# First output projection in seven products of quarters, with feed-forward weights, modulations and one delta product moved

## The chip, the cores and the metric

The kernel runs on one core of one Trainium2 chip. Its time is the device time of one execution in microseconds (us), and the median of three runs is given. TensorE (PE) multiplies matrices into PSUM, VectorE (DVE), ScalarE (ACT) and GpSimd (POOL) work on elements, and SP issues the DMA transfers. Everything is fp32. An engine works through its own instructions in order, and the engines wait for each other by semaphores.

## The reference

768 tokens (256 context, 512 latent) of 1024 features go through two layers of a diffusion transformer with different mixers, and then the latent tokens through a second block with a delta-rule mixer, latent attention and experts. The parts that the change touches, cut:

```python
for l in range(2):
    m = split((silu(c) @ mod_w[l] + mod_b[l]), 6)              # modulations
    h = rms(x, norm_pre_mix[l]) * (1 + m[1]) + m[0]
    o = even_mixer(h) if l == 0 else odd_mixer(h)              # l = 0: gated linear attention, softmax attention
    x = x + m[2] * rms(o @ w_out, norm_post_mix[l])            # output projection: out0, out1
    h = rms(x, norm_pre_ffn[l]) * (1 + m[4]) + m[3]
    x = x + m[5] * rms((silu(h @ w_gate[l]) * (h @ w_up[l])) @ w_down[l], norm_post_ffn[l])
# layer 1 is computed for the 512 latent tokens only; D_FF = 2816
```

## The kernel before

The features or tokens lie on 128 partitions; there are 6 tiles of 128 tokens (TILES), the first two context. The stages follow one another, each a block of instructions for all engines with tensors and semaphores of its own: opening, `even_mixer` (gla), `even_attention` (att), `closing` (out0), `gate_up` and `down` (ffn0), `odd_mixer` (hgrn), `closing` (out1), `gate_up` and `down` (ffn1), `delta_mixer` (dn), and the later ones up to the experts. A stage's instructions are issued only when the engine has left the stage ahead. An `Ahead` is a small buffer that an earlier stage's SP fills for a later one.

**`closing`** multiplies hT (features by tokens, 8 tiles of 128 features) with the output weights in the plain form: for each of 2 blocks of 512 columns and each of 6 token tiles, 8 products of 128x512 that add up in one bank (L633, L651). Behind the second block's products the tile two places back, which ScalarE and VectorE have normalised, is turned by 8 transpositions (L601), and its modulation is taken from PSUM by ScalarE (L685) and VectorE (L758).

**`down`** multiplies in seven products for eight (Strassen's, in Winograd's form), on quarters: a couple of token tiles by a pair of feature tiles of the weights (`lo`, `hi`) by two halves of the columns. In a step j TensorE issues the products 1, 6, 2, 7, 5, 4, 3 (L1235), each of 128x512, each into its own bank, over all steps of a couple. GpSimd makes two sums of each step's weights (L1298, L1299) and VectorE two more (L1323, L1325) and, for two steps at once, four sums of the operands (L1312 to L1317). At a couple's end VectorE collects the seven banks into the two tiles (L1329, seven adds), and in the steps of the next couple these are squared (ScalarE L1264), gated (L1353), added to the residual x (L1361), squared again (L1273), normalised (L1373), turned (TensorE L1206) and taken (L1283, L1380). The weights come by SP in steps of 1 MB into three homes. It has 11 steps a couple, `STEPS`.

**`gate_up`** does the same with quarters of 2816 hidden features, in units (gate and up by turns): products L960, GpSimd's sums L1018, L1019, L1023, VectorE's L1040, L1042, L1049, L1051.

**`even_attention`** runs 24 units of softmax attention. Twenty modulations (chunks of `mod_w`, 64 narrow products on TensorE, L2127, bias on VectorE, L2330) are spread over it, four of them ahead of the first scores (L2164), the rest at marks in the loop (`mod_at`). SP streams their weights in two homes (L2079) and stores all results at the end (L2089). The row sums of squares of q and k are products with a constant `att_two`, brought by DMA (L2136).

**`delta_mixer`** runs 10 periods of 6 chunks n; in period p the inputs of head p are projected (L3324) while chunks of earlier heads go through the recurrence. z0 (L3373) multiplies masked matrices dn_W with the identity, ScalarE copies the result to Z (L3676) and VectorE adds (`right`, L3775).

## Time and profile before

| | us |
|---|---|
| median of 3 runs (4270.95, 4272.61, 4286.95) | 4272.61 |
| the profiled execution's own time / its span | 4270.7 / 4268.9 |
| attention stage (att) | 307.5 to 504.9 |
| first output projection (out0) | 504.9 to 602.0 |
| gate and up, layer 0 / down, layer 0 | 602.0 to 1008.2 / 1008.2 to 1234.3 |
| hgrn, out1 | 1234.3 to 1781.2 |
| gate and up, layer 1 / down, layer 1 | 1781.2 to 2080.3 / 2080.3 to 2240.3 |
| delta mixer and later | 2240.3 to 4268.9 |

A stage's start is read from the first DMA issue of its SP in the timeline. In the timeline a row is: start, duration, engine, line, operation, what it writes <- what it reads, shapes, number of instructions put together, and in brackets how long the engine had been idle before and what ended it. A fp32 product is two records, so "x24" of products are 12 instructions. PEld is the load of the stationary operand beside the products. A wait row says which engine's instruction waited for which, total us, how often, and the longest. Idle time of an engine other than TensorE matters only if TensorE, or SP's loads, wait for it. PEclk is the granted clock of TensorE, 1.00 is full.

### The profile page before, as it was taken

How to read it: one execution, taken by the hardware profiler on the slowest of the kernel's cores; microseconds unless marked ns; L12 is line 12 of the kernel's file. 1: busy time of each engine (PE TensorE's matmuls, PEld its weight loads, DVE VectorE, ACT ScalarE, POOL GpSimd, SP SyncE). 2: the span in 40 equal slices, each digit the busy share in tenths (PEclk: the TensorE clock that was granted, in tenths of full speed). 3: DMA queues.
4: the chain of work that ended last, by engine and by line, in shares of the span. 5: the costliest groups of instructions: out<-in, count | busy, mean ns of one | idle time of the engine just before them, and what ended most of it. 6: DMA issues, size and time to landing. Idle time of an engine off the chain costs nothing. (4 is left out here: it accounts for less than half of the span.)

```text
span 4268.9 us, 51405 instructions
## 1 busy us (share of the span) xinstructions
PE 3946.4 (92%) x20867; PEld 2419.5 (57%) x20867; DVE 1673.3 (39%) x3130; ACT 852.4 (20%) x1663; POOL 690.8 (16%) x513
## 2 busy tenths in 40 slices
PE   7997889999999999899989899989998898999988
PEld 4665545554458666588646666767654445443333
DVE  2346442234764554533473555543124224111111
ACT  3224320000121332200013333321123211000000
POOL 0003212223420111122332232310002200000000
PEclk8998999999999999999998999999999998999999
DMA  4107511113532110253332010004200224999999
GB/s 172 40 24 270 194 40 59 59 60 114 173 108 60 30 45 32 107 217 139 133 128 54 21 31 23 21 34 139 81 1 1 116 79 169 406 421 422 422 421 369
DMA packets 323409, 580.12 MB, mean 136 GB/s; under 512 B 58876, under 2 KB 189404, under 8 KB 322536
## 3 DMA queue, kind: packets, MB, share of 16 engines
q1 hardware_dynamic: 323176, 576.84, 36.9%
q8 instruction: 168, 2.75, 0.3%
q14 instruction: 65, 0.53, 0.0%
HBM read 566.15 MB, written 10.63 MB: 135 GB/s over the span
## 5 line engine op out<-in xcount | busy, mean ns | idle before, releaser
L3324 PE MATMUL dn_ps<-room,dn_w 128*128 128x512 f32 (+1 forms) x616 | 229.6, 526 | 5.2 <-DVE dn_qx L3862 3.5
L960 PE MATMUL ffn_up_ps<-room,ffn_up_w 128*128 128x384 f32 (+1 forms) x704 | 208.8, 440 | 12.7 <-DMA ffn_up_w<-in_ffn_w_gate 12.7
L960 PE MATMUL ffn_up_ps<-ffn_up_t,room 128*128 128x384 f32 (+1 forms) x704 | 204.0, 433 | 1.2 <-DVE room L1040 1.2
L960 PE MATMUL ffn_up_ps<-room 128*128 128x384 f32 (+1 forms) x704 | 203.9, 432 | 0.0
L4870 PE MATMUL experts_ps<-experts_ring,experts_xs 128*64 128x512 f32 (+1 forms) x768 | 162.2, 573 | 25.3 <-DMA experts_ring<-in_w_up 25.3
L960 PEld LDWEIGHTS ffn_up_ps<-room,ffn_up_w 128*128 128x128 f32 x704 | 134.9, 193 | 71.9 <-DMA ffn_up_w<-in_ffn_w_gate 13.5
L3324 PEld LDWEIGHTS dn_ps<-room,dn_w 128*128 128x128 f32 x616 | 117.0, 195 | 96.0 <-issue 82.4
L2634 PE MATMUL hgrn_ps<-room,hgrn_w 128*128 128x512 f32 x372 | 170.3, 593 | 0.9 <-DVE hgrn_v L2888 0.9
L4870 PE MATMUL experts_ps<-experts_ring,room 128*64 128x512 f32 (+1 forms) x768 | 160.9, 569 | 8.7 <-DMA experts_ring<-in_w_up 8.1
L960 PEld LDWEIGHTS ffn_up_ps<-ffn_up_t,room 128*128 128x128 f32 x704 | 133.8, 190 | 57.4 <-DVE room L1040 1.9
L960 PEld LDWEIGHTS ffn_up_ps<-room 128*128 128x128 f32 x704 | 133.8, 190 | 55.7
L1235 PE MATMUL ffn_down_ps<-ffn_down_w_sums,ffn_down_hid_sums 128*128 128x512 f32 x330 | 161.8, 599 | 2.3 <-DVE ffn_down_w_sums L1323 2.3
L1047 DVE TENSOR_TENSOR room<-ffn_up_ps,room 128x384 f32<-128x384 f32 (+1 forms) x154 | 73.4, 489 | 222.2 <-PE ffn_up_ps L960 222.2
L4964 DVE TENSOR_TENSOR x_sb<-x_sb,experts_ps 128x512 f32<-128x512 f32 x56 | 38.5, 688 | 297.9 <-PE experts_ps L4805 297.9
L4920 PE MATMUL experts_ps<-experts_ring,experts_hidT 128*64 128x512 f32 x616 | 135.5, 594 | 10.2 <-issue 6.0
L4870 PEld LDWEIGHTS experts_ps<-experts_ring,experts_xs 128*64 128x64 f32 x768 | 58.6, 140 | 130.0 <-issue 126.7
L651 PE MATMUL out_ps<-out_w,room 128*128 128x512 f32 x296 | 131.0, 601 | 0.8 <-ACT room L699 0.8
L1235 PE MATMUL ffn_down_ps<-ffn_down_w,ffn_hid 128*128 128x512 f32 x220 | 116.5, 612 | 15.3 <-DMA ffn_down_w<-in_ffn_w_down 14.5
L1018 POOL TENSOR_TENSOR room<-ffn_up_w 128x512 f32<-128x512 f32 x44 | 56.7, 1288 | 440.3 <-PE ffn_up_ps L960 233.3
L1323 DVE TENSOR_TENSOR ffn_down_w_sums<-ffn_down_w,ffn_down_w_sums 128x512 f32<-128x512 f32 x55 | 82.0, 1490 | 95.7 <-POOL ffn_down_w_sums L1298 95.7
L4870 PEld LDWEIGHTS experts_ps<-experts_ring,room 128*64 128x64 f32 x768 | 54.5, 139 | 109.8 <-issue 108.2
L1235 PEld LDWEIGHTS ffn_down_ps<-ffn_down_w_sums,ffn_down_hid_sums 128*128 128x128 f32 x330 | 63.4, 193 | 84.4 <-issue 83.0
(665 smaller groups left out, 7176.7 us busy)
## 6 DMA issues: line engine op xcount, KB each, us to landing
experts_ring<-in_w_gate SPq DMA_DIRECT2D x128, 704.0 KB, 14.2
experts_ring<-in_w_up SPq DMA_DIRECT2D x128, 704.0 KB, 17.4
experts_ring<-in_w_down SPq DMA_DIRECT2D x160, 512.0 KB, 13.0
ffn_down_w<-in_ffn_w_down SPq DMA_DIRECT2D x55, 1024.0 KB, 4.9
att_wm<-in_mod_w SPq DMA_DIRECT2D x20, 2048.0 KB, 9.3
ffn_up_wm<-in_ada_w SPq DMA_DIRECT2D x12, 2048.0 KB, 12.5
ffn_up_w<-in_ffn_w_up SPq DMA_DIRECT2D x22, 1024.0 KB, 7.6
ffn_up_w<-in_ffn_w_gate SPq DMA_DIRECT2D x20, 1024.0 KB, 5.4
```

The source lines that it names most:

```text
L651: mm = nc.tensor.matmul(ps[:, u % BANKS, 0:wd], xT[:, k, t * P:(t + 1) * P], wt[:, j % ring, k, 0:wd], start=k == 0, stop=k == kt - 1)
L960: mm = nc.tensor.matmul(result(n, p), lhs[:, k, :], rhs[:, k, :], start=k == 0, stop=k == half - 1)
L1018: nc.gpsimd.tensor_tensor(s[:, 0, :, :], quarter(n, 1, lo), quarter(n, 1, hi), ALU.add).then_inc(S["s1_done"], 1)
L1047: nc.vector.tensor_tensor(kept(n, to), result(n, p), kept(n, q), ALU.add).then_inc(done, 1)
L1235: mm = nc.tensor.matmul(result(p, prod), lhs, rhs, start=j == 0, stop=j == STEPS - 1)
L1323: nc.vector.tensor_tensor(t[:, 1, :], hi[:, right], t[:, 0, :], ALU.subtract).then_inc(S["t2_done"], 1)
L2634: mm = nc.tensor.matmul(ps[:, bank, :], weights(j, k)[:, piece * P:(piece + 1) * P], hT[:, k, CTX:], start=k == 0, stop=k == KD - 1)
L3324: mm = nc.tensor.matmul(out, ahead.tile[:, k, :] if k < by_ahead else wt[:, h % 2, piece, k, :], hT[:, k, tok], start=k == 0, stop=k == KD ...
L4870: mm = nc.tensor.matmul(ps[out_rows, 3 * n + c, 0:b - a], xs_now[:, j, at:at + SLOTS], ring[:, w_at + a:w_at + b], start=j == 0, stop=j == ...
L4920: mm = nc.tensor.matmul(ps[out_rows, 6 + half, :], hidT[:, f, out_rows], ring[:, w_at:w_at + 512], start=f == 0, stop=f == FT - 1)
L4964: nc.vector.tensor_tensor(dst, dst, ps[:, bank, :], ALU.add).then_inc(S["scatter_out"], 1)
```

## The change

Four parts.

1. **out0** is computed by `down` instead of `closing`, with 4 steps a couple (`short`): couples (0,3), (1,4), (2,5). The weights, 4 MB, are streamed once for each couple, three DMAs a step. Of the first step only the low half is brought by the stage ahead. Turnings stand at other steps, and VectorE's schedule in a couple is a new one.
2. **Feed-forward weights.** `front` (the first gate weights) is loaded at the end of out0 and out1, and `gate_up` brings the first two steps of `down` (`next_load`, waited for as `early_in`) once its last block but one is multiplied. For this the homes of the weights are shared between `gate_up` and `down`.
3. **Attention.** Three modulations instead of four open the stage: two ahead of the first scores, one behind the second. One more stands at the end, after the last pair's values. The constant is made by VectorE, and the reductions for the scan's norm stand ahead of VectorE's wait for the key's factors.
4. **Delta mixer.** z0 and the copy of it move from the end of a period (n = 5) to the start of the next, behind `out_of`; z0 and two sums of squares use bank 5.

```diff
+    STEPS = hid.shape[1] // 2
+    short = STEPS < 10
+    if short:
+        turn_after = {(2, 1): (0, 0), (2, 5): (0, 1), (3, 2): (1, 0), (3, 5): (1, 1)}
+    GATES_AT = 3 if short else 8
...
+                        if beside and (j, at_order) in turn_after:
+                            which, part = turn_after[j, at_order]
+                            turn(p, beside[which], part)
...
+                    if short and beside:
+                        one, other = beside
+                        if j == 0:
+                            mean_y(one)
+                            gated(one)
+                            mean_y(other)
+                            residual(one)
+                            gated(other)
+                        elif j == 1:
+                            mean_x(one)
+                            residual(other)
+                            normed(one)
+                        elif j == 2:
+                            mean_x(other)
+                            normed(other)
+                        else:
+                            take(p, one)
+                            take(p, other)
+                        continue
...
-    closing(nc, "out0", hT, KD, out0_jobs, x, mix, hT, ident,
-            (mods[0], 2, I["norm_post_mix"][0]), (I["norm_pre_ffn"][0], mods[0], 3, 4), ahead=out0)
+            down(nc, "out0", hT, None, x, mix, hT, ident, (mods[0], 2, I["norm_post_mix"][0]), (I["norm_pre_ffn"][0], mods[0], 3, 4), front.load, small[:, :],
+                 [out0_w[:, n, :] for n in range(3)], out0_w[:, 3, :], [], 0, fetch=out0_fetch, ahead=out0)
...
 # gate_up
         def weights_here(eng, n):
             if n == 0:
-                eng.wait_ge(S["lo_in"], 16)
-            eng.wait_ge(S["w_in"][2 * ((n // 2) % 2) + n % 2], 16 * (n // 4 + 1))
+                eng.wait_ge(front.sem, 16)
+            else:
+                eng.wait_ge(S["w_in"][n % 4], 16 * (n // 4 + (1 if n % 4 else 0)))
...
+            sp.wait_ge(S["product"], 7 * 2 * (blocks - 1))
+            next_load(sp)
...
 # even_attention
-    OPENING, LOOP = 4, 4
+    OPENING, LOOP = 3, 4
+    OPENING_BANKS = (3, 6)
...
-        return (0, 1, 3, 4) if j + 1 < PAIRS else (0, 1, 2, 3)
+        return (0, 1, 3, 4) if j + 1 < PAIRS else (0, 1, 2, 3, 4)
...
-            for m in range(OPENING):
-                modulated(m, m)
+            for m, bank in enumerate(OPENING_BANKS):
+                modulated(m, bank)
...
+                if u == 0:
+                    modulated(len(OPENING_BANKS), OTHER)
...
 # delta_mixer, TensorE, ScalarE, VectorE
+                else:
+                    side("z0", hi)
...
-                elif n == 5:
-                    side("z0", hp)
...
+                    if hi is not None:
+                        act.wait_ge(S["side"], side_n["z0", hi])
+                        nc.scalar.copy(Z[:, :, :], blocks(5)).then_inc(S["z_start"], 1)
...
+                if n == 0:
+                    right(0, hi)
...
-                    right(0, hp)
```

TensorE's order in out0, before: the plain products, with turnings behind the last blocks (out0_ps is the stage's PSUM, cst holds the identity).

```order
L651 MATMUL out0_ps<-out0_w,room 128x512 x60
L601 MATMUL out0_ps<-cst,room 128x128 x8
L651 MATMUL out0_ps<-out0_w,room 128x512 x8
L601 MATMUL out0_ps<-cst,room 128x128 x8
L651 MATMUL out0_ps<-out0_w,room 128x512 x8
L601 MATMUL out0_ps<-cst,room 128x128 x8
L651 MATMUL out0_ps<-out0_w,room 128x512 x8
L601 MATMUL out0_ps<-cst,room 128x128 x24
```

After, in steps three and four of the second couple (out_w_sums holds the sums of weights and, as the stationary operand, those of hT):

```order
L1259 MATMUL out_ps<-out_w 128x512
L1259 MATMUL out_ps<-out_w,room 128x512
L1259 MATMUL out_ps<-out_w_sums,out_w 128x512
L1229 MATMUL out_ps<-cst,room 128x128 x4
L1259 MATMUL out_ps<-out_w,room 128x512
L1259 MATMUL out_ps<-out_w_sums,out_w 128x512 x2
L1259 MATMUL out_ps<-out_w_sums,room 128x512
L1229 MATMUL out_ps<-cst,room 128x128 x4
L1259 MATMUL out_ps<-out_w 128x512
L1259 MATMUL out_ps<-out_w,room 128x512
L1259 MATMUL out_ps<-out_w_sums,out_w 128x512
```

A tile is now turned in two halves between single products, and the products before and behind need sums of the same step.

TensorE's order at the seam of two periods of the delta mixer, before:

```order
L3404 MATMUL dn_ps<-dn_LT,dn_Y 64x64 x12
L3433 MATMUL dn_ps<-room,dn_T 128x128 x2
L3373 MATMUL dn_ps<-cst,dn_W 64x64 x12
L3461 MATMUL dn_ps<-dn_state,dn_qT 128x256
L3463 MATMUL dn_ps<-room,dn_qk 128x128 x2
```

After:

```order
L3479 MATMUL dn_ps<-dn_LT,dn_Y 64x64 x12
L3508 MATMUL dn_ps<-room,dn_T 128x128 x2
L3536 MATMUL dn_ps<-dn_state,dn_qT 128x256
L3538 MATMUL dn_ps<-room,dn_qk 128x128 x2
L3536 MATMUL dn_ps<-dn_state,dn_qT 128x256
L3538 MATMUL dn_ps<-room,dn_qk 128x128 x2
L3448 MATMUL dn_ps<-cst,dn_W 64x64 x12
L3399 MATMUL dn_ps<-room,dn_w 128x512 x8
```

z0 (dn_W) has moved behind the four products of the outputs and stands right ahead of the projection.

## Rows read from the trace of the kernel before

**Rows 1.** Page, part 1: busy us (share of span) and instructions by engine.

```profile
PE 3946.4 (92%) x20867; PEld 2419.5 (57%) x20867; DVE 1673.3 (39%) x3130; ACT 852.4 (20%) x1663; POOL 690.8 (16%) x513
```

**Rows 2.** TensorE's waits to 2300: for what; us in total, times, longest.

```profile
PE ffn_down_ps L1235 <- DMA ffn_down_w<-in_ffn_w_down: 14.5, 2, 7.4
...
PE ffn_up_ps L960 <- DMA ffn_up_w<-in_ffn_w_gate: 12.7, 2, 6.4
...
PE att_ps L2127 <- DMA att_wm<-in_mod_w: 7.8, 2, 6.1
```

**Rows 3.** TensorE's waits in the delta mixer, 2240 to 3000.

```profile
PE dn_ps L3373 <- DVE dn_W L3846: 15.1, 8, 4.5
...
PE dn_ps L3324 <- DVE dn_qx L3862: 3.5, 6, 0.6
```

**Rows 4.** Timeline, z0: start, us, engine, line, operation, out<-in, count, [idle <-releaser].

```profile
2301.20 1.55 PE L3373 MATMUL dn_ps<-cst,dn_W 64*64 64x64 f32 x24 [3.36 <-DVE dn_W L3846]
```

**Rows 5.** Timeline of the attention stage's opening.

```profile
330.20 3.79 SPq L2079 DMA_DIRECT2D att_wm<-in_mod_w  x2
...
331.45 1.93 PE L2127 MATMUL att_ps<-att_wm,conditions 128*2 128x128 f32 x64
...
332.94 0.69 DVE L2344 TENSOR_TENSOR even_raw<-att_tmp 128x512 f32<-128x512 f32 x1
...
339.52 3.59 PE L2127 MATMUL att_ps<-att_wm,conditions 128*2 128x128 f32 x64 [6.14 <-DMA att_wm<-in_mod_w]
...
349.55 2.85 PE L2164 MATMUL att_ps<-even_raw 64*128 64x256 f32 x16 [1.36 <-issue]
...
356.44 1.12 PE L2196 MATMUL att_ps<-cst,att_probs 128*128 128x128 f32 x4 [4.04 <-DVE att_probs L2405]
```

**Rows 6.** Timeline of the attention stage's end.

```profile
495.95 3.97 SPq L2089 DMA_DIRECT2D mod<-att_mod  x8
...
496.07 5.37 PE L2213 MATMUL att_ps<-att_pT,even_av 128*64 128x512 f32 x24 [0.81 <-DVE att_mod L2330]
```

**Rows 7.** SP's waits, 300 to 620.

```profile
SPq L44 <- DMA mod<-att_mod: 1.4, 1, 1.4
```

**Rows 8.** Windows: from:to, us, busy us (instructions) by engine, PEclk, DMA share, GB/s.

```profile
505.00:602.00 97.00, 89.15 (x240) 42.41 (x240) 34.08 (x82) 27.33 (x73) 0.00 (x0) 0.97 0.20 55
1024.00:1076.00 52.00, 52.00 (x123) 23.06 (x122) 29.93 (x36) 0.00 (x0) 22.32 (x18) 1.00 0.61 211
1081.00:1147.10 66.10, 65.95 (x166) 29.98 (x165) 48.27 (x71) 9.65 (x22) 28.17 (x21) 1.00 0.50 166
```

**Rows 9.** Timeline of the first down projection's start.

```profile
1008.27 0.42 DVE L1312 TENSOR_TENSOR ffn_down_hid_sums<-ffn_hid 128x256 f32<-128x256 f32 x1 [1.82 <-PEq L47]
...
1013.23 2.07 PE L1235 MATMUL ffn_down_ps<-ffn_down_w,ffn_hid 128*128 128x512 f32 x2 [7.44 <-DMA ffn_down_w<-in_ffn_w_down]
...
1014.48 1.26 POOL L1299 TENSOR_TENSOR ffn_down_w_sums<-ffn_down_w 128x512 f32<-128x512 f32 x1
1014.55 1.74 DVE L1323 TENSOR_TENSOR ffn_down_w_sums<-ffn_down_w,ffn_down_w_sums 128x512 f32<-128x512 f32 x1 [4.72 <-POOL ffn_down_w_sums L1298]
...
1016.43 2.05 PE L1235 MATMUL ffn_down_ps<-ffn_down_w_sums,ffn_down_hid_sums 128*128 128x512 f32 x2 [1.13 <-DVE ffn_down_w_sums L1323]
...
1023.56 1.02 PE L1235 MATMUL ffn_down_ps<-ffn_down_w,ffn_hid 128*128 128x512 f32 x2
```

**Rows 10.** The same, later: an operand sum beside GpSimd.

```profile
1102.63 1.43 DVE L1312 TENSOR_TENSOR ffn_down_hid_sums<-ffn_hid 128x256 f32<-128x256 f32 x1
```

**Rows 11.** The same stage's end.

```profile
1228.71 3.48 PE L1206 MATMUL ffn_down_ps<-cst,room 128*128 128x128 f32 x16 [8.27 <-DVE room L1373]
```

**Rows 12.** Timeline of the first gate-and-up stage's start.

```profile
602.01 1.76 DVE L1049 TENSOR_TENSOR ffn_up_t<-room 128x1536 f32<-128x1536 f32 x1 [1.14 <-PEq L47]
...
605.83 5.22 PE L960 MATMUL ffn_up_ps<-room,ffn_up_w 128*128 128x384 f32 x8 [6.37 <-DMA ffn_up_w<-in_ffn_w_gate]
...
610.89 2.74 PE L960 MATMUL ffn_up_ps<-ffn_up_t,room 128*128 128x384 f32 x8
```

More of the change, by code:

```diff
@@ L1081, in _, with down @@
                         ins.then_inc(S["mod_out"], 1)
-def down(nc, tag, hid, w, x, y, hT, ident, gate, norm, then, small, tile0=0, before=None):
+def down(nc, tag, hid, w, x, y, hT, ident, gate, norm, then, small, raw, hsum, early_in, tile0=0, before=None, fetch=None, ahead=None):
     mod_g, gate_at, gain = gate
     gain_n, mod_n, shift_at, scale_at = norm
-    STEPS = DFF // P // 2
+    STEPS = hid.shape[1] // 2
[3 more added lines that the diff above has]
+    else:
+        turn_after = {(6, 6): (0, 0), (7, 6): (0, 1), (8, 6): (1, 0), (9, 6): (1, 1)}
+    GATES_AT = 3 if short else 8
     half = D // 2
@@ L1163, in tokens, with pieces, low, high @@
             return slice((t - tile0) * P, (t - tile0 + 1) * P)
+        def pieces(n):
+            j = n % STEPS
+            if fetch is None:
+                return [(raw[n % RAW], w.rearrange("(k p) n -> p k n", p=P)[:, j::STEPS, :])]
+            return fetch(raw[n % RAW], j, 1 if ahead and n == 0 else 0)
+        arrived, so_far = [], [0] * RAW
+        for n in range(n_pairs * STEPS):
+            if n >= len(early_in):
+                so_far[n % RAW] += 16 * len(pieces(n))
+            arrived.append(so_far[n % RAW])
+        def low(n):
+            return ahead.tile[:, 0, :] if ahead and n == 0 else raw[n % RAW][:, 0, :]
+        def high(n):
+            return raw[n % RAW][:, 1, :]
         @block.sync
         def _(sp):
-            v = w.rearrange("(k p) n -> p k n", p=P)
             def weights(n):
@@ L1192, in weights_here @@
         def weights_here(eng, n):
-            eng.wait_ge(S["w_in"][n % RAW], 16 * (n // RAW + 1))
+            if n < len(early_in):
+                eng.wait_ge(early_in[n], 16)
+            else:
+                eng.wait_ge(S["w_in"][n % RAW], arrived[n])
+                if ahead and n == 0:
+                    eng.wait_ge(ahead.sem, 16)
         @block.tensor
@@ L2047, in even_attention @@
         n_mod = len(chunks)
-        assert n_mod == OPENING + LOOP * PAIRS
+        assert n_mod == OPENING + sum(len(mod_at(j)) for j in range(PAIRS))
         wm = sb("wm", 2, KD, 512)
@@ L2344, in rope @@
                 nc.vector.tensor_tensor(lat, tmp[:, 0, :], tmp[:, 1, :], ALU.add).then_inc(S["roped"], 1)
+            for a in range(2):
+                for b in range(2):
+                    nc.vector.memset(two[a * DH:(a + 1) * DH, b:b + 1], 1.0 if a == b else 0.0).then_inc(S["two_set"], 1)
             dve.wait_ge(S["const_in"], CONSTS)
@@ L3048, in first_block, with out0_fetch @@
     gla = Ahead(first, loaded[0], I["even_w_in"][0].rearrange(by_feature, p=P)[:, :, E_Z:E_Z + 2 * GLA_RANK])
-    out0_jobs = columns(I["even_w_out"][0], range(TILES), rows=pair_rows)
-    out0 = Ahead(first, loaded[1], out0_jobs[0][0][0][0][1][:, 0:2, 0:512])
+    out0_rows = pair_rows(I["even_w_out"][0])
+    (_, scan_rows), = out0_rows[0]
+    out0 = Ahead(first, loaded[1], scan_rows[:, 0:1, :])
+    def out0_fetch(dst, j, have):
+        return [(dst[parts, half:half + 1, :], rows[:, j:j + 1, :]) for half in range(have, 2) for parts, rows in out0_rows[half]]
     hgrn = AheadPieces(first, loaded[0], [I["odd_w_in"][0].rearrange(by_feature, p=P)[:, 0:2, i * D:i * D + P] for i in range(3)])
@@ L3372, in side @@
                         for side, rows in enumerate(sides_of):
[L3373 removed]
+                            mm = nc.tensor.matmul(block_of(5, side, c), W[rows, h % 2, c, :], ident[rows, rows], start=True, stop=True)
                 mm.then_inc(S["side"], 1)
```

154 lines of the change are left out of this document (81 added, 73 removed).

## The prediction

> **What bounds the kernel now.** I read the busy times of the page first. TensorE works 3946 of 4269 us [rows 1], so the other engines matter only where TensorE waits for them, and the time can fall in two ways only: less work for TensorE, or fewer of its waits. Then I read its waits up to the end of the first block [rows 2]: 14.5 us for the first weights of the two down projections, 12.7 us for those of the two gate-and-up projections, and 7.8 us for the modulation weights of the attention stage. In the delta mixer, 15.1 us stand at one small product, called z0 below [rows 3]. The change aims at each of these. The experts behind all this run at the rate of their weights, but their loads wait for the stages ahead, so what is won or lost earlier reaches the end in full. What has to be asked of each wait is what TensorE would wait for next.
>
> **Attention stage, opening.** Now four modulations stand ahead of the first scores. Two ran without a wait; the other two stand right before the scores and wait 7.8 us for their weights [rows 2], the first for 6.14 us after a load issued at 330.20. The scores come at 349.55, and the first transposition of probabilities at 356.44, so the chain maximum, exponential, sum, normalisation takes 6.9 us [rows 5]. After the change only the two modulations without a wait stand ahead of the scores. The last rope on VectorE ends at 333.6 [rows 5], and six reductions that stood behind it now stand ahead of it, in a stretch where VectorE waited. So the scores start at about 334. GpSimd's gating now lies beside the chain, for which I add 2 us. The first transposition comes at about 334 + 6.9 + 2 = 342.9, which is 13.5 us earlier (bounds 12 and 15.7). The third modulation stands behind the scores, and its weights land at 339.5 as now, just ahead of that.
>
> **Attention stage, end.** One modulation of 64 products is moved to the very end, behind the products of the last values. Those start at 496.07 and take 5.37 us [rows 6], so it starts at 501.4. It needs 0.7 for its bank, 1.9 for itself (the 64 products at 331.45 took that [rows 5]) and 1.2 for VectorE to add the bias: 505.2. Only then may SP store all modulations. It does so now at 495.95 in 3.97 us, beside those products, and waits 1.4 us for their landing [rows 6, 7]. After: 505.2 + 0.5 + 3.97 + 1.4 = 511.1, where the next stage begins at 504.9 now. That is 6.2 us later. The store had been covered by the products, and that cover is gone. Together the attention stage gives 13.5 - 6.2 = **7.3 us** back.
>
> **First output projection.** Now the stage takes 97.0 us, with 96 matmul instructions (each two records of the trace) and TensorE busy for 89.2 [rows 8]. After: 3 couples x 4 steps x 7 = 84. One step of seven lasts 66.1 / 11 = 6.01 us, from the second couple of the first down projection, which runs the same function and in which TensorE is busy for 65.95 of 66.10 us [rows 8]. So the products take 84 x 0.858 = 72.1 us, 10.3 less than 96 of them. But the function has a start and an end. The first down projection takes 226.1 us for 33 steps, so 226.1 - 33 x 6.01 = 27.8 us are overhead: the DMA wait (5 us from the stage's start), the wait for the first sums (3.2 us), the slow clock of its start (the first product takes 2.07 us where it takes 1.02 later), the transpositions of four tiles inside, and at the end 8.3 us until the last couple is normalised and 5.6 more to turn it [rows 9, 11]. That gives 72.1 + 27.8 = 99.9, already 3 us more than now. The old form turned its tiles beside products of other tiles.
>
> Then VectorE. In the down projection it has 11 steps to finish a couple of tiles beside the next, here 4. In the 52.0 us ahead of the first collection it is busy 29.93 us with sums alone: 29.93 / 52.0 x 6.01 = 3.46 us a step. In the 66.1 us of a couple with normalisation it is busy 48.27, so the rest is 48.27 - 11 x 3.46 = 10.2 us [rows 8]. Here a couple has 4 x 3.46 + 10.2 = 24.0 us of VectorE beside 4 x 6.01 + 1.7 = 25.7 us of TensorE. It is 93% full, and most of its work is a chain with ScalarE and GpSimd, where it can't be packed. An operation that has to wait for GpSimd is long: the same sum of operands takes 0.42 us alone and 1.43 us beside GpSimd [rows 9, 10]. I laid the operations of couples two and three out one behind the other with these durations. The product of the third step waits 3.3 us for its weight sums, which stand behind the mean, gate and residual of the tiles; the first turning waits 2.2 us for the normalised tile, the second 2.7 us for VectorE to take the first, and 0.5 is left at a step. The second couple comes to 8.6 us of waits, the third to 5.4. At the end the last collection begins behind the second take: 4.9 us more, of which about 1 is won back, since no long wait stands ahead. Sum: 99.9 + 8.6 + 5.4 + 4.9 - 1 = 117.8, so **+20.8 us** (bounds +3 if every wait is hidden, +30 if the clock falls in them).
>
> The rule on the two engines can be weighed. The weight sum at 1014.55 is recorded with 1.74 us beside GpSimd's of 1014.48, which ends at 1015.74 [rows 9]. The Trainium skill, in "SBUF — State Buffer", section "Who interferes with whom", says that a VectorE operation with two SBUF inputs and a GpSimd operation that reads SBUF exclude each other, and the one that issues second waits until the first is done. By that rule 0.69 us behind 1015.74 would end at 1016.4, and the trace has 1016.3, so it agrees. Without the rule, with 0.68 us for each of these, VectorE would have some 4 us less a couple, and the stage would come to about 108 us.
>
> **Weights ahead of the feed-forwards.** The waits for DMA fall away, but the product right behind is bound by sums, not by weights. In the first gate-and-up stage the weights come at 605.83, and the first product on a sum at 610.89, though the stage begins at 602.0: 8.9 us [rows 12]. VectorE's first operand sum, which ran alone under that wait, takes 1.76 us [rows 12]. After, two of these and the weight sums, 1.3 us and more each, start together and take turns: 6.3 us if VectorE comes first, 10.0 if GpSimd does, 8.15 between them. So 0.75 us less, and I give the second such stage, with four tiles for six, the same: **-1.5** (bounds -12.7, if the sums cost nothing, and +4). For the down projections the first sum is used 8.2 us after the start (1008.27 to 1016.43). Now four operand sums of 0.42 us run while the weights are awaited [rows 9]; after they take turns with GpSimd at 1.43 [rows 10], and the product comes after about 6.8 us with a DMA that has long landed. Later steps gain no more, since the slow clock at the start stays. I take **-1.5** for both (bounds -14.5 and 0). The early loads themselves run beside products in stages where the DMA engines have room.
>
> **Delta mixer.** z0 waits for VectorE's masks eight times, 15.1 us in all [rows 3]; the first two periods hold 3.4 [rows 4] and 4.5 of it, and there nothing else is ready, so they stay. The other six are 7.3 us. Behind it now come the outputs of the period before, then z0, then the projection, whose eight products of 0.86 hide ScalarE's copy and VectorE's first use. The sums of squares move to a bank of their own, which frees the projection of a wait of 3.5 us [rows 3], and the copy of z0 does so for 1.1. Less 0.7 for one wait that the last period gains: 11.2. Since such waits partly come back at the next chain (neighbours of z0 wait in the same period), I take **-10** (bounds -4 and -16).
>
> **Sum.** Against the profiled execution's own time of 4270.7 us: -7.3 + 20.8 - 1.5 - 1.5 - 10 = +0.5, so 4271. The median of the runs is 2 us higher, which I leave out. Forecast: **4271 us, no change** (about 0.5%, 21 us either way, is what a measurement of this kernel can tell from none).
>
> **Rivals.**
> A. The weights ahead pay in full: TensorE's 12.7 and 14.5 us go, since one of the two summing engines gets through first and the clock recovers earlier. Then 4271 - 24 = 4247. For it: those rows name the DMA and nothing else. Against: sums that start with the stage take 6.3 us at best.
> B. VectorE's work in the short stage is hidden better than laid out, by a luckier order of turns: out0 at 104 us, 4271 - 14 = 4257. With A it would be 4233. For it: VectorE is at 93%, not over 100.
> C. Slower. Place: couples two and three of the first output projection. VectorE's chain, not TensorE, sets each step, and TensorE's clock falls in the gaps as it does at the start of the down projection. One slow stretch in each couple costs 5 us, ten us of products at 2.07 for 1.02 us [rows 9]. A couple takes 25.7 + 7 = 32.7 us in my sum; one of 39 costs 13 more over both: 4271 + 10 + 13 = 4294. It decides from a couple of 38 us on.
> D. Attention and delta mixer give nothing, because the waits move to the next chain: 4271 + 17 = 4288.
>
> **How the numbers follow.** Chances: forecast 0.45, B 0.17, A (with or without B) 0.20, D 0.10, C 0.08. Range: 4244 to 4290, which leaves out most of C, a little of D and A with B in full. Faster (below 4251): A and some of B, 0.22. Slower (above 4292): C and the tail of D, 0.09. No change: 0.69.
>
> **What would show it.** In the profile after: the stage from the attention's last product to the first gate-and-up product at 115 to 121 us, TensorE waiting there on VectorE's weight sums and on its taken tiles, and a last wait of 12 us ahead of the last turning; the first transposition of probabilities 13 us earlier and the store of the modulations behind the last product; no DMA wait at the four feed-forward stages but 6 to 10 us to the first product on a sum; z0 without a wait in six of eight periods. I am wrong if out0 stays under 108 us, or if the four starts take under 4 us.

## The result: 0.5% slower, where no change was forecast

The changed kernel takes 4300.6 us (median of 5 runs, 4295.24 to 4303.42), the kernel before, run as often, 4273.9. The ratio is 1.0053, with a 95% interval of 1.0043 to 1.0064. The profiled execution's span is 4299.6 us at a mean clock of 0.954 (before 4268.9 at 0.960), 30.7 us more. My range ended at 4290.

A stage lasts from its SP's first DMA issue to the next stage's. All tables below are read that way from the timeline of SP.

| stage | before | after | difference | forecast |
|---|---|---|---|---|
| up to attention | 307.4 | 306.8 | -0.6 | |
| attention | 197.4 | 193.5 | -3.9 | -7.3 |
| out0 | 97.1 | 127.5 | +30.4 | +20.8 |
| gate and up 0 / down 0 | 406.3 / 226.1 | 410.1 / 225.3 | +3.8 / -0.8 | -0.75 / -0.75 |
| hgrn / out1 | 465.6 / 81.3 | 465.5 / 81.5 | -0.1 / +0.2 | |
| gate and up 1 / down 1 | 299.1 / 160.0 | 299.7 / 159.1 | +0.6 / -0.9 | -0.75 / -0.75 |
| delta mixer | 663.0 | 660.6 | -2.4 | -10 |
| its projections / mla | 119.7 / 359.7 | 119.5 / 362.9 | -0.2 / +3.2 | |
| mix / wo to the end | 126.9 / 759.3 | 125.8 / 761.7 | -1.1 / +2.4 | |

### The profile page after: what moved, and what is told of

Its sections match the earlier page's. It is cut to its first block and busy times, and to the rows that moved or that the text cites. A ratio compares the mean times of both kernels' runs of the same rounds, so it can differ in the third digit from the quotient of the medians.

```text
span 4299.6 us, 51462 instructions
## 1 busy us (share of the span) xinstructions
PE 3965.8 (92%) x20843; PEld 2425.4 (56%) x20843; DVE 1732.6 (40%) x3191; ACT 852.5 (20%) x1654; POOL 727.7 (17%) x537
## 5 line engine op out<-in xcount | busy, mean ns | idle before, releaser
L961 PE MATMUL ffn_up_ps<-ffn_up_t,room 128*128 128x384 f32 (+1 forms) x704 | 208.4, 440 | 10.2 <-DVE room L1037 10.2
L1259 PE MATMUL ffn_down_ps<-ffn_down_w_sums,ffn_w 128*128 128x512 f32 x330 | 163.2, 604 | 10.8 <-DVE ffn_down_w_sums L1347 10.8
L961 PE MATMUL ffn_up_ps<-room,ffn_w 128*128 128x384 f32 (+1 forms) x512 | 148.8, 434 | 0.0
L961 PEld LDWEIGHTS ffn_up_ps<-room,ffn_w 128*128 128x128 f32 x512 | 97.0, 190 | 41.2 <-issue 1.1
L1259 PEld LDWEIGHTS ffn_down_ps<-ffn_down_w_sums,ffn_w 128*128 128x128 f32 x330 | 63.9, 194 | 92.2 <-issue 90.8
L3772 POOL TENSOR_TENSOR dn_LT<-dn_W,cst 128x384 f32<-128x384 f32 x48 | 47.9, 997 | 376.9 <-DVE dn_W L3858 337.0
L4996 PEld LDWEIGHTS experts_ps<-experts_ring,experts_hidT 128*64 128x64 f32 x616 | 51.0, 138 | 89.0 <-issue 89.0
L1715 PE MATMUL gla_ps<-gla_w,room 128*128 128x384 f32 x288 | 100.0, 501 | 0.0
L2682 PEld LDWEIGHTS hgrn_ps<-room,hgrn_w 128*128 128x128 f32 x372 | 66.0, 191 | 59.8 <-issue 59.5
## 6 DMA issues: line engine op xcount, KB each, us to landing
ffn_up_wm<-in_ada_w SPq DMA_DIRECT2D x12, 2048.0 KB, 12.5
```

The costliest lines, as they stand in the source:

```text
L961: mm = nc.tensor.matmul(result(n, p), lhs[:, k, :], rhs[:, k, :], start=k == 0, stop=k == half - 1)
L1259: mm = nc.tensor.matmul(result(p, prod), lhs, rhs, start=j == 0, stop=j == STEPS - 1)
L1715: mm = nc.tensor.matmul(ps[:, bank, 0:wd], hT[:, k, t * P:(t + 1) * P], wt[:, s, k, 0:wd], start=k == 0, stop=k == KD - 1)
L2682: mm = nc.tensor.matmul(ps[:, bank, :], weights(j, k)[:, piece * P:(piece + 1) * P], hT[:, k, CTX:], start=k == 0, stop=k == KD - 1)
L3772: nc.gpsimd.tensor_tensor(LT[:, :, :], W[:, h % 2, :, :], small(SMALL_HALVES + n + 1), ALU.mult).then_inc(S["lt_done"], 1)
L4996: mm = nc.tensor.matmul(ps[out_rows, 6 + half, :], hidT[:, f, out_rows], ring[:, w_at:w_at + 512], start=f == 0, stop=f == FT - 1)
```

## The profile after

Waits of TensorE up to 2300 in the changed kernel (engine, tile, line, awaited: total us, times, longest). They answer [rows 2].

```profile
PE out_ps L1229 <- DVE room L1397: 12.4, 1, 12.4
...
PE ffn_down_ps L1259 <- DVE ffn_down_w_sums L1347: 10.8, 2, 5.4
PE ffn_up_ps L961 <- DVE room L1037: 10.2, 2, 6.7
PE out_ps L1259 <- DMA out_w<-in_even_w_out: 9.6, 1, 9.6
...
PE out_ps L1259 <- DVE room L1353: 4.3, 1, 4.3
...
PE out_ps L1229 <- DVE room L1404: 2.8, 1, 2.8
```

No row is left of the 27 us of waiting for the weights of the feed-forwards. In their place stand 10.8 and 10.2 us for sums by VectorE (L1347, L1037). out0 has waits that it did not have before: 12.4 at its end, 9.6 at its start (4.6 of it inside the stage, which begins at 500.22), 4.3 for the first collection, 2.8 for a taken tile.

The start of the first gate-and-up stage after the change, from the timeline, answers [rows 12]:

```profile
627.79 2.87 DVE L1046 TENSOR_TENSOR ffn_up_t<-room 128x1536 f32<-128x1536 f32 x1 [0.74 <-PEq L47]
627.79 2.82 PE L961 MATMUL ffn_up_ps<-room,ffn_front 128*128 128x384 f32 x8 [2.15 <-PEq L47]
...
631.74 4.93 POOL L1020 TENSOR_TENSOR room<-room 128x1536 f32<-128x1536 f32 x1
633.32 3.90 DVE L1037 TENSOR_TENSOR room<-room,ffn_front 128x512 f32<-128x512 f32 x1
...
637.27 5.49 PE L961 MATMUL ffn_up_ps<-ffn_up_t,room 128*128 128x384 f32 x8 [6.66 <-DVE room L1037]
```

The weights are there, and product 1 runs at once. Then TensorE waits 6.66 us. VectorE's two operand sums and s2 (L1037), and GpSimd's t3 (L1020, 4.93 us) take turns, and product 6 comes 9.5 us after the start, later than the 8.9 us of before. It then takes 5.49 us, where the same product took 2.74 before [rows 12]: the clock is still down.

out0, the second couple and the last turning, from the timeline of the changed kernel:

```profile
535.40 4.49 DVE L1424 TENSOR_TENSOR out_gate<-out_gate,room 128x1024 f32<-128x1024 f32 x2
536.57 2.24 POOL L1323 TENSOR_TENSOR out_w_sums<-out_w 128x512 f32<-128x512 f32 x1
539.92 4.53 DVE L1353 TENSOR_TENSOR room<-out_ps,room 128x512 f32<-128x512 f32 x7
...
540.67 1.77 PE L1259 MATMUL out_ps<-out_w,room 128*128 128x512 f32 x2 [4.30 <-DVE room L1353]
...
542.24 2.97 PE L1259 MATMUL out_ps<-out_w_sums,out_w 128*128 128x512 f32 x4
...
558.54 1.09 PE L1229 MATMUL out_ps<-cst,room 128*128 128x128 f32 x4 [3.59 <-issue]
```

```profile
570.68 0.68 PE L1229 MATMUL out_ps<-cst,room 128*128 128x128 f32 x4 [2.76 <-DVE room L1404]
...
595.77 1.09 PE L1229 MATMUL out_ps<-cst,room 128*128 128x128 f32 x4 [3.59 <-issue]
...
622.00 3.65 PE L1229 MATMUL out_ps<-cst,room 128*128 128x128 f32 x16 [12.37 <-DVE room L1397]
```

The two products of gates and gain (L1424) take 4.49 us beside GpSimd and stand ahead of the collection (L1353, 539.92), so TensorE waits 4.30 us at 540.67. Behind it two records take 1.77 and four 2.97 us, where two take 1.02 and four 1.88 at full clock. The same happens behind 558.54 (a wait of 3.59), 570.68 (2.76) and 595.77 (3.59).

## Experiments

Twelve kernels were run. A ratio is to the kernel before on the same chip. Where a kernel ran only once (early_late, warm, sched, fill, end_first, before_again), I go by the lengths of the stages. hgrn, which no edit touches, took 465.3 to 465.6 us in 11 of 14 traces and 464.9 to 466.9 in all. Other stages vary more without an edit: p34_only has 301.5 and 227.3 us in the second gate-and-up and the first down stage, where the kernel before had 299.1 and 226.1. Attention varies by 5 us from trace to trace, and the delta mixer once by 3.7 (fill). So a difference of 1 or 2 us between two stages says little by itself.

| stage | p34_only | p2_only | p1_off | p34_off | early_late | warm | sched | fill | end_first | best1 | best2 |
|---|---|---|---|---|---|---|---|---|---|---|---|
| attention | 191.2 | 202.1 | 192.0 | 200.0 | 189.7 | 190.4 | 191.9 | 192.9 | 194.7 | 194.9 | 192.4 |
| out0 | 98.6 | 97.1 | 99.7 | 128.3 | 123.4 | 126.4 | 114.5 | 124.2 | 112.1 | 99.7 | 99.8 |
| gate, up 0 | 405.7 | 409.2 | 409.6 | 410.1 | 405.6 | 407.1 | 403.9 | 403.9 | 403.9 | 407.5 | 403.8 |
| down 0 | 227.3 | 224.9 | 225.1 | 225.3 | 224.7 | 222.8 | 224.4 | 225.4 | 223.8 | 222.8 | 222.8 |
| gate, up 1 | 301.5 | 299.3 | 299.3 | 299.7 | 295.9 | 298.0 | 295.9 | 295.9 | 295.9 | 297.4 | 295.6 |
| down 1 | 160.5 | 159.4 | 159.7 | 159.1 | 159.2 | 158.2 | 159.2 | 159.4 | 159.2 | 157.2 | 157.2 |
| delta mixer | 659.4 | 663.6 | 660.1 | 663.6 | 660.7 | 659.7 | 660.6 | 664.3 | 660.6 | 661.1 | 659.5 |
| mla | 363.0 | 363.0 | 363.0 | 363.0 | 362.8 | 362.9 | 362.9 | 362.8 | 362.8 | 363.0 | 363.1 |

### The parts one by one

**p1_off**: out0 in the plain form again.

```diff
-            down(nc, "out0", hT, None, x, mix, hT, ident, ...)
+        closing(nc, "out0", hT, KD, out0_jobs, x, mix, hT, ident, ..., ahead=out0, then=front.load)
```

> The changed kernel with the first output projection in the plain form again; the other three parts stay. Theory T (the loss is out0's own, 127.5 us against 97.1, and the other parts add up to about zero): out0 takes 97 us again, the kernel 4270 us, the gate-and-up stage behind it still 3 to 4 us longer than before. Rival R1 (the loss lies partly in what out0 leaves behind, the slow clock with which the next stage starts): out0 gives back 30, and the next stage 4 more, so 4266 us.

Measured: 4269.6 us (10 runs, 4266.41 to 4275.54), ratio to before 0.9984 (0.9974 to 0.9993). out0 takes 99.7 us. The loss of the whole change is out0's, 28 us by the stages and 31 by the medians. The gate-and-up stage behind it stays at 409.6, so R1 falls: that stage's loss is its own.

**p34_off**: attention and delta mixer as before, the rest as changed (both functions taken whole from the kernel before).

> The changed kernel with the attention stage and the delta mixer as before. Theory T (by the stages of the two traces, attention is worth 3.6 us and the delta mixer 2.4): the kernel takes 4306 us, with an attention stage of 197.4 and a delta mixer of 663. Rival R2 (both are worth what was forecast, 7 and 10, and something else in the changed kernel hid it): 4316 us or more.

Measured: 4309.2 us (4 runs, 4304.94 to 4312.97), 1.0073 (1.0056 to 1.009), with 200.0 and 663.6 us in the two stages. Both parts gain. The time lies between the two expectations, nearer to theory T's 4306.

**p34_only**: the kernel before with the two functions of the change.

> The kernel before with only the changed attention stage and the changed delta mixer. Theory T (attention is worth about 7 us, as 199.5 against 192 in the mean of the traces so far, the delta mixer 2.5): 4276.5 - 9.5 = 4267 us. It also tells where the 3.3 us of latent attention (mla, 359.7 in both traces of before, 362.9 in all six of changed kernels, at the same waits) come from: 359.7 here if they belong to the weights ahead, 362.9 if they belong to the delta mixer or to any shift of the program. Rival R2 (the attention gain is run-to-run variation of that stage): 4272 us or more.

Measured: 4267.0 us (10 runs, 4260.3 to 4273.4), 0.9977 (0.9968 to 0.9986), where theory T had 4267; it had counted on 9.5 us less than the kernel before, and on this chip it is 7.4 less (4274.4). Attention is 191.2. Over all traces, the old form takes 197.4, 201.7, 202.1 and 200.0, the new one 189.7 to 194.9 (ten traces), so some 8 us; the trace after the change, with 193.5, showed less than the usual gain. mla takes 363.0 here too.

**p2_only**: the kernel before with the feed-forward weights ahead.

> The kernel before with only the feed-forward weights ahead (with GpSimd's order as in the change). By the stages of p1_off: gate-and-up +3.4 and -0.5, out0 up to +2.6, down -1 and +0.5, mla +3.2 if it belongs to it. Theory T (the DMA wait is exchanged for a wait on sums and a longer slow clock, so the 27 us of DMA waits give nothing): 4276.5 + 3 to 8, about 4282 us. Rival A of the prediction (the waits for DMA come through in full): 4250 us.

Measured: 4278.4 us (10 runs, 4273.85 to 4282.36), 1.0007 (0.9998 to 1.0016). 27 us of DMA waits are gone from the trace and nothing is gained; the interval holds 1. Rival A falls. The four stages stand at 409.2, 224.9, 299.3 and 159.4: together 1.3 us more than before.

### What stands behind the starts

**early_late**: two edits in stages apart.

```diff
-    GATES_AT = 3 if short else 8
+    GATES_AT = 2 if short else 8
...
             weight_sums(0)
-            pool.wait_ge(S["t1_done"], 1)
+            pool.wait_ge(S["s2_done"], 1)
             nc.gpsimd.tensor_tensor(t3, b22, b12, ALU.subtract)
```

> The changed kernel with two edits in stages that do not touch. In out0 VectorE multiplies the gates one step earlier, at the third step of the first couple. In both gate-and-up stages GpSimd makes the operand sum t3 only behind VectorE's first weight sum s2. Theory T (VectorE was late for the first collection because of the gates, and s2 because it took turns with t3): TensorE's wait of 4.3 us in out0 ahead of the second couple goes and out0 falls from 127.5 to about 123; the first product on a sum of the gate-and-up stage comes 6 us after the start where it came after 9.5, and the stage is 3 us shorter. Rival R3 (collection and s2 are late for the many sums as such): out0 stays within 1 us of 127.5, and the wait only moves to the turnings; the gate-and-up stage stays at 410.

Measured: out0 123.4 (-4.1), the two gate-and-up stages 405.6 and 295.9 (-4.5 and -3.8). TensorE's wait ahead of product 6:

```profile
627.00 4.54 PE L961 MATMUL ffn_up_ps<-ffn_up_t,room 128*128 128x384 f32 x8 [1.85 <-DVE room L1037]
```

Product 6 comes 6.25 us after the start of 620.75, with 1.85 us of waiting for s2 left in the row. One wait, moved on GpSimd, brings 8.3 us in two stages. So theory T holds for both edits: s2 was late because it took turns with t3, and the gates stood ahead of the collection.

**warm**: product 1 repeated at the starts.

```diff
+                        for again in range(3 if n == 0 and prod == 1 else 0):
+                            nc.tensor.matmul(result(p, prod), lhs, rhs, start=True, stop=True)
                         mm = nc.tensor.matmul(result(p, prod), lhs, rhs, start=j == 0, stop=j == STEPS - 1)
```

> The changed kernel with more products at three starts, results thrown away: in the gate-and-up stages the first unit's product 1 is made three times, in the down stages and out0 the first step's product 1 four times. It tests whether the slow clock behind the starts comes from TensorE's idle gap of 5 to 7 us there. Theory T (the gap costs twice, once itself and once as products at half the clock behind it; with TensorE busy in the gap the clock is full when the sums are there): product 6 of the first gate-and-up stage takes 2.7 us instead of 5.5, and the stage is 3 to 5 us shorter, each down stage 2 to 4 us shorter. Rival R4 (the clock comes back only some time after the stage's start, whatever TensorE does): the stages keep their length within 1 us, or get longer by the added products.

Measured, against the changed kernel: down 222.8 and 158.2 (-2.5, -0.9), gate and up 407.1 and 298.0 (-3.0, -1.7), out0 126.4 (-1.1). The start of the first down stage, from TensorE's timeline, in the changed kernel and in warm:

```profile
1037.91 1.10 PE L1259 MATMUL ffn_down_ps<-ffn_w,ffn_hid 128*128 128x512 f32 x2 [2.60 <-PEq L47]
...
1044.38 2.05 PE L1259 MATMUL ffn_down_ps<-ffn_down_w_sums,ffn_w 128*128 128x512 f32 x2 [5.38 <-DVE ffn_down_w_sums L1347]
...
1046.22 1.92 PE L1259 MATMUL ffn_down_ps<-ffn_w,ffn_hid 128*128 128x512 f32 x2
...
1047.93 2.71 PE L1259 MATMUL ffn_down_ps<-ffn_down_w_sums,ffn_w 128*128 128x512 f32 x4
```

```profile
1031.20 2.81 PE L1263 MATMUL ffn_down_ps<-ffn_w,ffn_hid 128*128 128x512 f32 x6 [2.60 <-PEq L47]
1033.85 1.02 PE L1264 MATMUL ffn_down_ps<-ffn_w,ffn_hid 128*128 128x512 f32 x2
1037.68 1.10 PE L1264 MATMUL ffn_down_ps<-ffn_down_w_sums,ffn_w 128*128 128x512 f32 x2 [2.81 <-DVE ffn_down_w_sums L1352]
1038.62 1.02 PE L1264 MATMUL ffn_down_ps<-ffn_w,ffn_hid 128*128 128x512 f32 x2
1039.48 1.88 PE L1264 MATMUL ffn_down_ps<-ffn_down_w_sums,ffn_w 128*128 128x512 f32 x4
```

In the changed kernel TensorE waits 5.38 us after one product, and the next take 2.05, 1.92 and 2.71 us. In warm it makes three more products, whose result nobody uses, waits 2.81 us, and the same ones take 1.10, 1.02 and 1.88. The wait was paid twice. R4 falls at this start, which is 2.5 us shorter. The 0.9 us of the second down stage would fit R4 too; in best1 and best2, with the same repeated products, that stage takes 157.2, 1.9 less than in the changed kernel. In the gate-and-up stage product 6 starts at 633.59, 9.5 us after the start, as in the changed kernel, and takes 2.85 for 5.49 us, as theory T had it.

### Inside out0

**sched**: early_late, and in out0

```diff
-        turn_after = {(2, 1): (0, 0), (2, 5): (0, 1), (3, 2): (1, 0), (3, 5): (1, 1)}
+        turn_after = {(2, 3): (0, 0), (2, 6): (0, 1), (3, 2): (1, 0), (3, 5): (1, 1)}
...
+                    if short and beside and j == 3:
+                        take(p, beside[0])
                     if n + 1 < n_pairs * STEPS:
```

> As early_late, and in out0 the first turning of a couple stands two products later, and VectorE takes the first turned tile ahead of the next couple's sums, behind which it had stood. Theory T (the waits of 2.8, 2.8 and 0.7 us come from the place of the turning and from that order on VectorE, and each of the long ones costs another 1.5 to 1.8 us of slow clock): the waits go down to about 1, the slow stretches behind them go too, and out0 takes 111 to 116 us instead of 123.4. Rival R3 (VectorE has too much to do in a short couple, so that the lateness only moves): 121 or more.

Measured: out0 114.5 us. Its longest waits from 530 on:

```profile
551.28 1.76 PE L1259 MATMUL out_ps<-out_w_sums,out_w 128*128 128x512 f32 x2 [3.20 <-DVE out_w_sums L1347]
...
584.97 0.68 PE L1229 MATMUL out_ps<-cst,room 128*128 128x128 f32 x4 [1.88 <-issue]
...
609.63 3.59 PE L1229 MATMUL out_ps<-cst,room 128*128 128x128 f32 x16 [12.37 <-DVE room L1397]
```

The 2.76 us for the taken tile are gone and the turnings wait less; R3 falls. The slow stretches, which theory T wanted gone, are partly left: one wait of 3.20 us for a weight sum remains in the second couple, and both it and the 1.88 us in the third have slow products behind them. The next two behind the 1.88 us take 1.68 and 1.91 us for 1.02.

**end_first**: sched, and the last couple's collection ahead of the last take.

```diff
-                        else:
+                        elif p < n_pairs - 1:
                             take(p, other)
...
                 collect(p)
+                if short and p == n_pairs - 1:
+                    take(p, beside[1])
```

> As sched, and for the last couple of out0 VectorE collects the products first and takes the last turned tile afterwards. Theory T (the 12.4 us of waiting ahead of the last turnings are 8 of normalising, as in the down stage, and 4 because the collection stands behind that take): the wait is 8.3 to 9 us and out0 takes 110 to 111 us instead of 114.5. Rival: the collection is slow for another reason, and the wait stays at 12.

Measured: the wait ahead of the last turnings falls from 12.37 to 10.66, not to 8.3, and out0 to 112.1. The order explains a part of the 4 us. What holds the other 2.4 stands in the trace:

```profile
597.09 0.59 ACT L1313 COPY room<-out_ps 128x512 f32<-128x512 f32 x1
...
597.71 4.53 DVE L1353 TENSOR_TENSOR room<-out_ps,room 128x512 f32<-128x512 f32 x7 [3.66 <-ACT room L1313]
```

VectorE's collection starts behind ScalarE's copy of the first bank (L1313), and that copy stands behind ScalarE's half of the take (L1307, 1.50 us from 595.70). So ScalarE's first square of the new tiles starts 3.16 us after the start of the last product (598.52 to 601.68); in the first down stage of the kernel before it was 1.33 us (1219.41 to 1220.74). That is 1.8 us. From there to the last turnings it is 8.52 us for 7.97, since VectorE's own take (1.36 us) now stands ahead of the mean: 0.6 us. A copy ahead of ScalarE's take was not tried.

**fill**: early_late, and four products, into the bank that the turning will use, ahead of the first turning of a couple.

```diff
+                            for again in range(4 if short and which == part == 0 else 0):
+                                nc.tensor.matmul(spare(p, 0), *operands[1], start=True, stop=True)
                             turn(p, beside[which], part)
```

> As early_late, and four products whose result is thrown away stand ahead of the first turning of the second and third couple, 3.4 us of work in the place of a wait of 2.85. Theory T (the wait itself brings the slow clock, 1.5 to 1.8 us each time): the products behind those two places run at full clock, and out0 takes 123.4 + 2 x 0.6 - 2 x 1.6, about 121.5 us. Rival R4 (the clock has another reason, the light transpositions for one): the slow stretches stay and out0 takes 124.5 us or more.

Measured: out0 124.2 us, neither expectation. The two couples went apart. In the second the order of VectorE and GpSimd fell otherwise, and TensorE waited 3.52 us earlier, for a weight sum, with slow products (2.05 us) behind; a later wait of 2.77 us has a slow stretch behind it too. In the third, no wait and no slow stretch is left at the turning, and from its first product to the last turnings it takes 42.8 us (576.08 to 618.89) where early_late takes 45.9 (569.03 to 614.95):

```profile
552.50 2.05 PE L1259 MATMUL out_ps<-out_w_sums,out_w 128*128 128x512 f32 x2 [3.52 <-DVE out_w_sums L1349]
...
576.08 1.10 PE L1259 MATMUL out_ps<-out_w,room 128*128 128x512 f32 x2 [0.69 <-DVE room L1406]
...
618.89 3.65 PE L1229 MATMUL out_ps<-cst,room 128*128 128x128 f32 x16 [12.37 <-DVE room L1399]
```

Of these 3.1 us, 1.1 are a shorter wait for a weight sum (0.33 for 1.41). The third couple speaks for theory T, the sum of both for nothing.

### A stage that nobody touched

**before_again**: the kernel before, profiled anew.

> The kernel before, profiled a second time. Two stages differ between traces for no edit: latent attention (mla) took 359.7 us in the trace of before and 363 in every trace since, though no line of it changed and its waits are the same, and the attention stage took 189.7 to 193.5 in the changed form. Theory V (the clock that TensorE is granted in these stretches varies from execution to execution, and the trace of before had luck): mla takes 362 to 363 here. Rival (the changed kernels do something to it): 359.7 again.

Measured: mla takes 359.7 again. So it isn't luck of one execution, and theory V falls. But the twelve changed programs, each profiled once, p34_only and p2_only among them, which share no edit, all take 362.8 to 363.1. The instructions start at the same time after the stage's start (146.15 us in before_again, 146.14 in p1_off) and then differ in nothing but the clock:

```profile
3173.56 1.55 PE L4095 MATMUL mla_ps<-cst 8*128 8x384 f32 x4
...
3175.04 2.84 PE L4058 MATMUL mla_ps<-mla_cqT,mla_big 128*128 128x512 f32 x6
```

```profile
3164.48 1.55 PE L4166 MATMUL mla_ps<-cst 8*128 8x384 f32 x4
...
3165.96 4.35 PE L4129 MATMUL mla_ps<-mla_cqT,mla_big 128*128 128x512 f32 x6
```

Six records of the same product take 2.84 us in one and 4.35 in the other, behind the same stretch of small products (8x384, 128x1) and with no wait in between. Set side by side, product by product, the two stages drift apart only between 146 and 155 us after the stage's start: by 1.5 us in these six records, and by the rest of the 3.3 in a few products behind them. What in the program decides it is open.

### A better kernel

**best1**: p1_off, t3 behind s2, and the repeated products at all four starts of the feed-forwards.

> The changed kernel with out0 in the plain form, t3 behind s2 on GpSimd, and product 1 repeated at the four starts of the feed-forwards. By the stages: p1_off took 4269.6; t3 took 4.5 and 3.8 us from the gate-and-up stages, the repeated products 2.5 and 0.9 from the down stages and 3.0 and 1.7 from the gate-and-up ones, where I expect a part to be the same microseconds. Theory T: 4269.6 - 8.3 - 3.4 - 1 = 4257 us, 0.4% faster than before. Rival R5 (at a start that already has its sums sooner, the repeated products only delay product 6): 4262 us.

Measured: 4265.9 us (9 runs, 4262.38 to 4267.54), 0.9975 (0.9965 to 0.9985). Theory T's 4257 is missed by 9 us, R5's 4262 by 4. R5 is right on the gate-and-up stages: 407.5 and 297.4, where early_late had 405.6 and 295.9.

**best2**: the same, with the repeated products in the down stages only.

> As best1, with the repeated products at the two down starts only. Theory T (at the gate-and-up starts, with s2 made ahead of t3, repeated products delay product 6: best1's stages took 407.5 and 297.4 where early_late had 405.6 and 295.9): 4265.9 - 2 - 1.5 = 4262 us. Rival R4: the same as best1, 4266.

Measured: 4257.4 us (5 runs, 4256.24 to 4260.33), 0.9958 (0.9944 to 0.9971): 17 us less than the kernel before and 43 less than the changed one. That is less than both expectations; the two gate-and-up stages give 5.5 us against best1, of 3.5 expected, and the kernel before is 2 us faster on this chip (4274.4 for 4276.5). The four stages are 403.8, 222.8, 295.6 and 157.2. Start of the first gate-and-up stage:

```profile
600.99 5.06 PE L961 MATMUL ffn_up_ps<-room,ffn_front 128*128 128x384 f32 x8 [2.55 <-PEq L47]
...
606.52 0.68 DVE L1037 TENSOR_TENSOR room<-room,ffn_front 128x512 f32<-128x512 f32 x1
...
607.25 2.85 PE L961 MATMUL ffn_up_ps<-ffn_up_t,room 128*128 128x384 f32 x8 [1.20 <-DVE room L1037]
607.27 3.94 POOL L1020 TENSOR_TENSOR room<-room 128x1536 f32<-128x1536 f32 x1 [2.30 <-DVE room L1037]
```

s2 (L1037) takes 0.68 us, since t3 (L1020) now starts behind it, and product 6 comes 6.3 us after the start at nearly full clock.

## Why the prediction was wrong, point by point

The sum missed by 30 us: out0 +9.6, gate and up +6.0, delta mixer +7.6, attention +3.4 in this trace, mla +3.2, down -0.2, the rest +0.6 (wo +2.4, mix -1.1 and small ones).

**Attention, right.** The first transposition of probabilities came 34.96 us after the stage's start (341.73 in a stage from 306.77), where it had come after 48.99: 14.0 us earlier, 13.5 forecast. The store of the modulations (494.01) stands beside the last, short products (494.13 to 495.2) and is no longer covered: from the last long products (484.75) to the next stage it is 15.5 us, where it was 8.8, so 6.7 are lost for 6.2 forecast. Between the two ends this trace lost another 3.4, within what the stage varies by. Of the gain some 8 us remain in the mean of the traces, 7.3 forecast. What I missed: the store leaves TensorE idle before out0, which then starts at a slower clock. In the plain form the first 24 product records take 12.06 us in p34_only and 13.11 in p1_off behind such an idle stretch of 5.1 us, and 10.54 in p2_only behind 1.1 us; the stage takes 98.6, 99.7 and 97.1. That is 1.5 to 2.6 us.

**out0, the place right, two terms put at nothing.** The step that failed is the one on VectorE's work. I laid out couples two and three only, with 10.2 us of other work from the down stage's second couple. The gates are multiplied in the first couple (in the down stage at its ninth step of eleven, with room behind), so they were in no term. Here they stand at its last step, right ahead of the first collection: 4.49 us, 4.30 of waiting, and 4.1 us less in early_late, where they stand one step earlier. The other waits of the couples were forecast at 14.0 and came to 11.0 (3.59, 2.76, 0.69, 0.34, 3.59); the 4.9 at the end were 4.1 (12.37 less 8.3). The second term is the clock: I counted no slow stretch inside the couples, but kept it for rival C. From 534.41 to 609.6 the products and turnings take 51.5 us at full speed, the listed waits 15.3; of the 8.4 left, 6.8 lie in the four slow stretches behind the long waits (1.8, 1.5, 1.8 and 1.7). With 4.3 and 6.8 added, and 3.8 taken off for the smaller waits, 117.8 becomes 125.1 of the 127.5. The second couple took 43.2 us (534.41 to 577.63), the third 31.8, 37.5 in the mean, and C was to decide from 38 on. So C, to which I gave 0.08, had the place and the clock that falls in the gaps. That VectorE's chain sets each step is not what the runs show: the third couple stayed under C's bound, and moving three operations (early_late, sched) took 13 of the 30 us. 2.4 us of the 127.5 stay unassigned.

**Weights ahead, the direction wrong for gate and up.** I put the two gate-and-up starts at -0.75 each, between 6.3 and 10.0 us, and it came to 9.5 us in the first: GpSimd's t3 was ahead of s2. That much was in the bounds. What wasn't is the clock: before, TensorE's product 1 (eight records) ran right ahead of product 6, which then had the full clock. After, product 1 runs early, TensorE stands still for 6.66 us, and product 6 takes 5.49 for 2.74. I had said for the down starts that "the slow clock at the start stays"; for these it got longer. For the two down stages -1.5 was forecast and -1.7 came, in part by luck: my own starts, 8.2 and 6.8 us, give 1.4 for each stage, so 2.8, of which I took about half without a reason. The first start came at 6.5 us (1044.38 in a stage from 1037.88).

**Delta mixer, the gain wrong.** The waits of z0 went where I said, six of eight (7.9 us are left, [rows 3] had 15.1):

```profile
PE dn_ps L3448 <- DVE dn_W L3923: 7.9, 2, 4.5
...
PE dn_ps L3536 <- ACT room L3666: 5.0, 7, 0.7
```

The step that failed is the one from these waits to the time: I took each microsecond of them for a microsecond of the period, less 1.2 of 11.2. Of one period, the rows at the seam, before and after:

```profile
2574.25 1.22 PE L3433 MATMUL dn_ps<-room,dn_T 128*128 128x128 f32 x4 [1.87 <-DVE room L3797]
...
2575.51 0.62 ACT L3591 ACTIVATE room<-dn_ps,dn_b 128x128 f32<-128x128 f32 x2 [1.82 <-PE dn_ps L3433]
...
2576.44 1.55 PE L3373 MATMUL dn_ps<-cst,dn_W 64*64 64x64 f32 x24 [0.96 <-DVE dn_W L3846]
2577.91 1.22 PE L3461 MATMUL dn_ps<-dn_state,dn_qT 128*128 128x256 f32 x2
...
2580.40 0.61 PE L3463 MATMUL dn_ps<-room,dn_qk 128*128 128x128 f32 x4
2580.84 7.03 PE L3324 MATMUL dn_ps<-room,dn_w 128*128 128x512 f32 x16
```

```profile
2601.29 1.22 PE L3536 MATMUL dn_ps<-dn_state,dn_qT 128*128 128x256 f32 x2 [0.71 <-ACT room L3666]
...
2604.01 1.06 PE L3538 MATMUL dn_ps<-room,dn_qk 128*128 128x128 f32 x4
2605.00 1.39 PE L3448 MATMUL dn_ps<-cst,dn_W 64*64 64x64 f32 x24
2606.32 7.13 PE L3399 MATMUL dn_ps<-room,dn_w 128*128 128x512 f32 x16
```

Before, ScalarE made the outputs' input (2575.51, 0.62 us) while TensorE waited 0.96 us for z0. After, the outputs come at once and wait for the same operation (0.71 us, L3666). The wait for z0 had covered another one. The outputs run wholly at the slow clock, 3.71 us (2601.29 to 2605.00) for 2.93 (2577.91 to 2580.84). So -0.96 (z0's wait) + 0.71 - 0.58 (the wait for a sum of squares, gone as forecast) + 0.78 - 0.15 (z0's own length) = -0.2 a period: 72.01 us from 2577.91 to 2649.92 before, 71.82 from 2601.29 to 2673.11 after. Six such periods give 1.2 us. The stage got 2.4 us shorter, where my smallest gain was 4.

**mla**, which I did not consider, is worth 3.2 us. The clock in a few of its products makes them up; why it differs is open.

## What to carry to other kernels

A wait for DMA is worth what TensorE would wait for next, and that is measured by the engines that also started on that DMA: bring their work ahead too, or order it by what the first product needs (one semaphore on GpSimd was worth 8 us here, the loads ahead alone nothing). A single product that is brought forward and followed by a gap can cost more than it gains, since the clock falls in the gap. Count each wait of 3 us or more inside a busy stage with a slow stretch behind it; below that it went either way here. Before a plain product is given to a scheme with fewer multiplications, compare its sums with the products of one step for the engine that has also to finish the tiles: 12.5% fewer products cost 30 us here and at best, in end_first, 15.

## What the runs showed of the hardware

In out0 of the changed kernel, each of four waits of 2.8 to 4.3 us between full-speed products was followed by 1.5 to 1.8 us lost to the clock. That a wait is paid again as slow products agrees with the Trainium skill, "TensorE: Matmul & The Clock Gate", section "HAM oscillation — how this bites in real kernels", which describes this for idle time that goes to waiting for DMA. The length alone doesn't decide. Behind the same wait of 2.76 us for a taken tile, two products took 3.10 us in the changed kernel (571.20) and 1.88 in early_late:

```profile
563.78 0.68 PE L1229 MATMUL out_ps<-cst,room 128*128 128x128 f32 x4 [2.76 <-DVE room L1404]
564.29 1.88 PE L1259 MATMUL out_ps<-out_w_sums,out_w 128*128 128x512 f32 x4
```

Behind the 2.81 us that were left at the down start in warm nothing was lost either, and behind 1.88 us in sched 1.7.

The same instructions at the same relative times can get another clock in another program (mla, 2.84 or 4.35 us). The kernel before had the same in both of its traces; every other program was profiled once.
